# A recurrent and attention block with its modulation moved beside matrix products, paired attention heads, and split top-k lists

## What is computed

```python
# first block: three branches, joined by one product
o = rms_norm(o, norm_g) * silu(z)                  # delta rule, 8 heads of 128
z5 = gelu(y_s5)                                    # state space, 512 channels
y_s5 = z5 * sigmoid(z5 @ s5_w_glu + b) * silu(s5_gate)
h = h + concat([y_rg, y_gdn, y_s5]) @ w_out        # 2048 -> 1024
gate = sigmoid(rms_norm(h, g) @ ple_w_gate)
h = rms_norm(h + gate * (p @ ple_w_proj), final_norm_g)
# delta rule, per chunk and head: a unit lower triangle is inverted
sol = triangular_solve(I + strict(K K^T * decay), rhs)
# modulation of two later layers, from a condition vector: scales, shifts and
# gates, one product of the condition with w_mod_2 (2 layers, 1024 x 6144)
# attention: 8 heads of 64 in two groups, each query block of 128 against three
# neighbouring key blocks and 256 context keys, with a sink in the softmax
# router of each expert layer: affinity = softmax(h @ w_router), 16 experts,
# and each expert takes its 128 highest tokens
```

## Time and profile before

| | us |
|---|---|
| three runs | 5097.38, 5098.56, 5117.61 |
| median | 5098.56 |
| the profiled execution (span 5129.8) | 5131.51 |

### The profile page before, as it was taken

How to read it: one execution, slowest core, us unless ns; L and a number is a source line. 1 busy time by engine, 2 the same in 40 slices (tenths; PEclk the granted TensorE clock), 3 DMA queues, 4 the chain that set the end, 5 groups by cost and what they waited for, 6 DMA issues and landing times. The chain is left out here.

```text
span 5129.8 us, 38618 instructions
## 1 busy us (share of the span) xinstructions
PE 4519.5 (88%) x14430; PEld 2352.2 (46%) x14430; DVE 1728.6 (34%) x3087; ACT 976.0 (19%) x1876; POOL 205.3 (4%) x235
## 2 busy tenths in 40 slices
PE   8999996586989699888687999997989995799996
PEld 3444443572444454558453444443444444344443
DVE  3545534554431331554544111112124245311111
ACT  3444431242010311351110000002000001000001
POOL 0011100000000000001000000000000000000000
PEclk9999998797989799897776999998999996899998
DMA  4122225356110121005237999972011112799995
GB/s 111 45 69 82 66 70 161 96 168 242 66 49 0 61 72 55 1 25 145 74 132 273 341 319 318 317 264 86 17 34 42 34 42 99 269 317 317 317 317 205
DMA packets 515952, 733.51 MB, mean 143 GB/s; under 512 B 114270, under 2 KB 228798, under 8 KB 515800
## 3 DMA queue, kind: packets, MB, share of 16 engines
q1 hardware_dynamic: 479032, 646.54, 37.0%
q0 software_dynamic: 11744, 43.00, 3.0%
q10 hardware_dynamic: 25024, 41.96, 2.3%
HBM read 655.40 MB, written 76.01 MB: 143 GB/s over the span
## 5 line engine op out<-in xcount | busy, mean ns | idle before, releaser
L2361 PE MATMUL ps<-ffn_w,moe_xT 128*128 128x512 f32 x2048 | 887.6, 594 | 3.3 <-DVE moe_xT L2422 3.3
L512 PE MATMUL ps<-hT,pr_w 128*128 128x512 f32 x1536 | 671.3, 595 | 5.0 <-issue 3.6
L2361 PEld LDWEIGHTS ps<-ffn_w,moe_xT 128*128 128x128 f32 x2048 | 390.3, 191 | 494.9 <-issue 490.8
L512 PEld LDWEIGHTS ps<-hT,pr_w 128*128 128x128 f32 x1536 | 290.6, 191 | 364.4 <-issue 361.7
L2377 PE MATMUL ps<-moe_w,moe_hT 128*128 128x512 f32 x1024 | 444.9, 592 | 0.1
L2435 DVE TENSOR_TENSOR moe_sg<-moe_sg,ps 128x512 f32<-128x512 f32 x64 | 44.0, 688 | 836.7 <-PE ps L2361 836.7
L2377 PEld LDWEIGHTS ps<-moe_w,moe_hT 128*128 128x128 f32 x1024 | 192.1, 190 | 230.1 <-issue 230.1
L2769 PE MATMUL ps<-hA,abp_w 128*128 128x512 f32 (+1 forms) x624 | 252.3, 565 | 0.6 <-DVE bv L2882 0.6
L2576 PE MATMUL ps<-hG,gmu_w 128*128 128x512 f32 x512 | 227.7, 603 | 4.8 <-DMA gmu_w<-in_gm_w_in 4.8
L2492 PE MATMUL ps<-gmv_w,hG 128*128 128x512 f32 x512 | 222.3, 597 | 10.2 <-DMA gmv_w<-in_gm_w_in 10.2
L2402 ACT ACTIVATE moe_sg<-ps 128x512 f32<-128x512 f32 x64 | 38.2, 597 | 1006.9 <-PE ps L2361 1006.9
(11 more groups left out here) (608 smaller groups left out, 5764.7 us busy)
## 6 DMA issues: line engine op xcount, KB each, us to landing
ffn_w<-in_moe_w_gate SPq DMA_DIRECT2D x64, 2048.0 KB, 10.3
ffn_w<-in_moe_w_up SPq DMA_DIRECT2D x64, 2048.0 KB, 9.1
moe_w<-in_moe_w_down SPq DMA_DIRECT2D x64, 2048.0 KB, 10.5
pr_w<-in_w_in SPq DMA_DIRECT2D x24, 1024.0 KB, 5.4
X<-in_w_mod ACTq DMA_DIRECT2D x10, 2048.0 KB, 9.8
route_modw<-in_w_mod ACTq DMA_DIRECT2D x10, 2048.0 KB, 8.1
X<-scratch_grow SPq DMA_DIRECT2D x48, 256.0 KB, 5.3
X<-scratch_k SPq DMA_DIRECT2D x32, 256.0 KB, 3.5
```

What stands on the lines that cost most here:

```text
L512: ins = eng.matmul(C.ps[r % NRING][:, :], w[:, (n // 2) % NW, k, (n % 2) * P:(n % 2 + 1) * P], HT[:, k, half * BANK:(half + 1) * BANK], st ...
L2361: ins = eng.matmul(C.ps[2 + b][:, :], xT[:, k, :], wb[b][:, k, :], start=(k == 0), stop=(k == KD - 1))
```

## The change

- The second elimination of `stage_gdn` is put on GpSimd; DVE does the first alone. GpSimd's copies are put on ACT. SP stores the first inverse and goes on to the loads, and stores the second before unit 8.
- `stage_gdn_out` and `stage_s5_out` are one stage, `stage_outs`. The reciprocal root is taken on ACT as exp(-0.5 ln(x)); the reciprocal on DVE is gone.
- `Modulation` is gone. `ModColumns` sums w_mod's rows, scaled by the condition, on DVE (96 instructions for a layer with one condition, 128 with two for four blocks), from 48 loads of 512 KB with two buffers, and turns each block to channels by products with one moving column. Layer 1 runs inside `wout`, layer 0 inside `ple`. The bank it needs leaves 7 to `wout`, and three tiles instead of four in flight to `ple`.
- `stage_attn` takes both groups in one pass: score products of the two groups on PE's rows 0 to 63 and 64 to 127, value products on its columns 0 to 63 and 64 to 127, five phases per query block, the division two and the transposes three query blocks behind.
- `stage_route` makes the router's product with 512 moving columns for the two halves of the tokens side by side, runs the rounds on 64 partitions by 512 tokens, and merges the two sorted lists of each expert by a product with a reversed identity and the larger of each pair.

```diff
--- before.py
+++ after.py
...
+            eng.wait_ge(s_al[1], 16)
+            step = Steps(eng, s_iv1)
+            for j in range(B - 1):
+                eliminate(eng, step, 1, j)
...
+            inverse_store(0)
             for u in range(4):
                 inverse_load(u)
             for u in range(4, NU):
+                if u == HU:
+                    inverse_store(1)
                 inverse_load(u)
                 rec_load(u)
...
+                eng.activation(X5[g][0:32, :, 32:64], AT[u][0:32, :, 32:64], ACT.Copy)
+                eng.activation(X5[g][64:96, :, 96:128], AT[u][64:96, :, 96:128], ACT.Copy).then_inc(s_X5, 1)
+
+            x5(0)
+            x5(1)
+            transposed(0)
...
+def stage_outs(nc, C, A, S, MIX, X):
...
+            def root(h):
+                r = rt[:, h % 2, :]
+                if h >= 2:
+                    eng.wait_ge(s_n, h - 1)
+                for half in range(2):
+                    eng.wait_ge(s_ss, 2 * h + half + 1)
+                    eng.activation(rt[:, h % 2, half_(half)], ssb(h, half), ACT.Ln, bias=C.eps[:, 0:1], scale=1.0 / P).then_inc(s_ln, 1)
+                eng.wait_ge(s_ln, 2 * h + 2)
+                eng.activation(r, r, ACT.Exp, scale=-0.5).then_inc(s_rt, 1)
...
+            square(0)
+            square(1)
+            for t in range(ST_):
+                gelu(t)
+            for h in range(HEADS):
+                root(h)
+                if h + 2 < HEADS:
+                    square(h + 2)
+                if h == HEADS // 2:
+                    eng.wait_ge(s_par, 32)
+                    sigmoid(0)
+                    sigmoid(1)
+            sigmoid(2)
+            sigmoid(3)
...
+            for h in range(5):
+                squares(h)
+            eng.wait_ge(s_w, 16)
+            eng.wait_ge(s_z, ST_)
+            glu(0)
+            glu(1)
+            for h in range(5, HEADS):
+                squares(h)
+            glu(2)
+            glu(3)
...
+class ModColumns:
+        for i in range(SHARE * KD // KQ):
+            u, kq = divmod(i, KD // KQ)
+            if i >= 2:
+                eng.wait_ge(self.s_used, i - 1)
+            eng.dma_start(self.parts[:, i % 2, :, :], A["w_mod_2"][l][kq * KQ * P:(kq + 1) * KQ * P, u * BANK:(u + 1) * BANK]
+                          .rearrange("(k p) c -> p k c", p=P)).then_inc(self.s_w[i % 2], 16)
...
+    def sums(self, eng):
+
+        for i in range(SHARE * KD // KQ):
+            u, kq = divmod(i, KD // KQ)
+            if u >= 2 and kq == 0:
+                eng.wait_ge(self.s_turned, u - 1)
+            eng.wait_ge(self.s_w[i % 2], 16 * (i // 2 + 1))
+            for k in range(KQ):
+                for r in range(self.rows(u)):
+                    w, a, c = self.parts[:, i % 2, k, :], self.acc[:, u % 2, r, :], self.C.cond[:, kq * KQ + k, r:r + 1]
+                    if kq == 0 and k == 0:
+                        ins = eng.tensor_scalar(a, w, c, None, ALU.mult)
+                    else:
+                        if r == 0 and k:
+                            eng.wait_ge(self.s_chain, i * (KQ - 1) + k)
+                        elif r == 0:
+                            eng.wait_ge(self.s_used, i)
+                        ins = eng.scalar_tensor_tensor(a, w, c, a, ALU.mult, ALU.add)
+                    if r == self.rows(u) - 1:
+                        ins.then_inc(self.s_chain if k < KQ - 1 else self.s_used, 1)
+                    yield
...
+    def turn(self, eng, u):
+
+        eng.wait_ge(self.s_used, KD // KQ * (u + 1))
+        n = BANK // P
+        for r in range(self.rows(u)):
+            for i in range(n):
+                o = (u * n + i) * 2 + r
+                ins = eng.matmul(self.C.ps[7][:, o:o + 1], self.acc[:, u % 2, r, i * P:(i + 1) * P], self.C.ones[:, 0:1], start=True, stop=True)
+        ins.then_inc(self.s_turned, 1)
...
+                    if md and 2 <= u < SHARE + 2:
+                        md.turn(eng, u - 2)
...
+                    if md and u < SHARE + 2:
+                        for _ in range(16 if u < 4 else 8):
+                            next(side, None)
+                    if md and u == SHARE + 2:
+                        md.finish(eng)
...
+PACE = (0, 2, 2, 2, 2, 2, 2)
...
+        nbk = 7 if md else 8
+        bank = lambda p, t: C.ps[(TH * p + t) % nbk][:, :]
...
+            def free(p, t):
+                q, t0 = divmod(TH * p + t - nbk, TH)
+                if q >= 0:
+                    eng.wait_ge(s_acc, nacc[q] + (t0 + 1) * len(SEVEN[q][2]))
...
+                        if md and p and k == 2:
+                            md.turn(eng, 2 * p - 1)
+                        if md and k == 6:
+                            md.turn(eng, 2 * p)
...
+                    if p:
+                        aside(PACE[p])
...
+                if md and p + 2 == NP:
+                    aside(SHARE * KD * 2)
+                    md.finish(eng)
...
+            for k in range(KD):
+                for half in range(2):
+                    ins = eng.matmul(C.ps[0][EQ * half:EQ * (half + 1), :], wr[:, k, :], HT[:, k, half * BANK:(half + 1) * BANK],
+                                     start=(k == 0), stop=(k == KD - 1), tile_position=(0, EQ * half))
...
             eng.wait_ge(s_t, 1)
-            for half in range(2):
-                step(eng.tensor_copy(affT[:, half * BANK:(half + 1) * BANK], C.ps[1 + half][0:E, :]))
+            step(eng.tensor_copy(affT[:, :], C.ps[2][0:HP, :]))
             for r in range(RND):
                 v8 = vals[:, 8 * r:8 * r + 8]
                 step(eng.max(v8, affT[:, :]))
                 step(eng.max_index(ixu[:, 8 * r:8 * r + 8], v8, affT[:, :]))
-                step(eng.match_replace(affT[:, :], v8, affT[:, :], -1.0))
+                if r + 1 < RND:
+                    step(eng.match_replace(affT[:, :], v8, affT[:, :], -1.0))
             eng.tensor_copy(ixf[:, :], ixu[:, :]).then_inc(s_top, 1)
...
+            eng.tensor_copy(lists[:, :, :], C.ps[3][:, 0:2 * HP].rearrange("p (a e) -> p a e", a=2)).then_inc(s_ls, 1)
+            eng.wait_ge(s_ls, 1)
+            eng.wait_ge(s_rv, 1)
+            near, nid = lists[:, 0, 0:E], lists[:, 1, 0:E]
+            fval, fid = C.ps[4][:, EQ:EQ + E], C.ps[4][:, HP + EQ:HP + EQ + E]
+            eng.tensor_tensor(won[:, :], near, fval, ALU.is_ge).then_inc(s_rv, 1)
+            step(eng.tensor_copy(idx[:, :], won[:, :]))
...
+                if x:
+                    for g in range(2):
+                        eng.matmul(bank[g][:, at * P:(at + nb) * P], S.bq[row[g], x - 1, qs], S.bk[row[g], lo * P:(lo + nb) * P],
+                                   start=True, stop=True, tile_position=(D_ * g, 0))
+                    for g in range(2):
+                        ins = eng.matmul(bank[g][:, LOC:], S.bq[row[g], x - 1, qs], S.kc[row[g], 0:P],
+                                         start=True, stop=True, tile_position=(D_ * g, 0))
+                else:
+                    for h in range(GH):
+                        for g in range(2):
+                            ins = eng.matmul(bank[g][:, h * P:(h + 1) * P], S.bq[row[g], h, qs], S.kc[row[g], P:],
+                                             start=True, stop=True, tile_position=(D_ * g, 0))
...
+            def values(z):
+                n, x = zs[z]
+                eng.wait_ge(s_cp, 2 * z + 2)
+                if x == 0 and n:
+                    eng.wait_ge(s_po, n)
+                for g in range(2):
+                    cs = slice(D_ * g, D_ * (g + 1))
+                    ins = eng.matmul(C.ps[7][cs, :], S.bv[:, keys(n)[x][1], cs], PT[z % 4][:, g, :],
+                                     start=(x == 0), stop=(z + 1 == z_end[n]), tile_position=(0, D_ * g))
...
+            for n in range(NT + LAG):
+                for x in range(NPH):
+                    if n < NT:
+                        scores(n, x)
+                    z = z_of.get((n - LAG, x))
+                    if z is not None:
+                        turn(z)
+                        if z:
+                            values(z - 1)
+            values(len(zs) - 1)
...
+            for n in range(NT + LAG):
+                for x in range(NPH):
+                    if x == 0 and n < NT:
+                        context(n)
+                    if x and 1 <= n <= NT:
+                        exps(n - 1, (2 * x - 2, 2 * x - 1))
+                    z = z_of.get((n - LAG, x))
+                    if z is not None:
+                        copies(z)
+                        if x == 1 and n > LAG:
+                            outputs(n - LAG - 1)
...
-        stage_gdn_out(nc, C, A, S, MIX, X, mod, cond, 0, SHARE)
-        stage_s5_out(nc, C, A, S, MIX, X, mod, gains)
-        stage_seven(nc, C, "wout", MIX, plain_rows(A["w_out"][0], 16), 16, X)
+        stage_outs(nc, C, A, S, MIX, X)
+        stage_seven(nc, C, A, "wout", MIX, plain_rows(A["w_out"][0], 16), 16, X, extra=(S, mod, gains, SHARE, 0))
...
```

(4 more changed lines are left out.)

777 lines of the change are left out of this document (376 added, 401 removed).

## The result

Four executions of the changed kernel took 4956.81, 4961.62, 4950.05 and 4944.85 us, median 4953.43; four of the kernel before 5097.38, 5098.56, 5117.61 and 5097.47, median 5098.02. The ratio is 0.9707, 95% interval 0.9678 to 0.9736: faster by 145 us. In a later comparison of four executions with seven the medians were 4956.24 and 5108.50, ratio 0.9695 (0.9668 to 0.9723). Forecast were 4895 us and a range of 4850 to 4945, so the direction held and the time did not: it lies 58 us above the forecast and 8 above the range. The profiled execution of after took 4956.81 us (span 4955.1), 174.7 us of span less than that of before.

A forecast was written before the change was run, and what follows sets the result against it. Stages bound separately: PE in `wout`, `ple` and attention, DVE's top-k in routers, reciprocals and modulation loads in ends, idle PE in `stage_gdn`. Terms -23 -84 +35 +27 -42 -43 -73 = -203; 5098.6 - 203 = 4895 us, range 4850 to 4945.

The forecast's parts named there:

- Inverse: In `stage_gdn`, PE starts 23.4 us earlier after the first store, with GpSimd's half covered: gain 23 us.
- Ends: In the end stages, ACT carries the chain at 6.05 us a head, DVE covered: 84 us against 168.1, gain 84.
- The drain: Rival in the end stages: every table load also drains, adding 26 us, total 4921; chance 0.04.
- rival of one table for logarithm and exponential: Rival in the end stages: both functions share one table, saving ACT some 18 us, total 4877; chance 0.03.
- `wout`: Loss 35 us: turns 15, first block's wait 10, banks 4, changeovers 3, half clock 3; bounds 12 and 60.
- `ple`: Loss 27 us: 20 sets of turns 19, PE's waits in the first four blocks 5, tail 3; bounds 15 and 60.
- rival that the loads become the clock: Rival: w_mod loads pace `wout` and `ple`, biting from 3.7 us a part; time 5110 or more; chance 0.04.
- Attention: Paired products overlap, the bound passes to PE, DVE and ACT at about 17 us a block: 165 us, gain 42.
- the rival: In the attention, score products of both groups do not overlap: 19.5 us per block, total 4922; chance 0.12.
- the case of 18 us: In the attention, tiling mode changes at an assumed 0.2 us each: PE holds 18 us a block, some 8 longer.
- Routers: Shorter top-k rounds and product gain 43 us in each router; the first also loses the modulation, gaining 73.
- The step to the median: Profiled execution lay 33 us above the median, so only the difference was taken: 5098.6 - 203 = 4895 us.

The follow-up runs named there:

- the experiment that takes the cover away: Kernel after with square root on ScalarE and reciprocal on VectorE again in the merged end stage: stage 106.1 us, total 4993.62 us.
- the experiment with pairs: Kernel after with the end stage's roots taken in pairs of heads, eight table loads fewer: stage 74.9 us, total 4939.66 us.
- the second profile: The kernel before, unchanged, profiled once more: 5119.98 us.

## Why the prediction was right or wrong, step by step

- **Inverse, -23 forecast, -11: wrong.** The steps behind the store held (PE 5.1 us after the first load; GpSimd 0.55 us an instruction against 0.61, done at 940.8, covered). The step that failed is "so PE starts 23.4 us earlier" (it was 14.6: 938.44 against 953.03), which took for granted that DVE's own half costs what it cost alone. With GpSimd beside it an instruction took some 600 ns instead of 363; started one after the other, DVE's half is back at its old length and 10.2 us are gained. Another 3.0 us are ScalarE's transposing copy (a period of 22.0 instead of 19.0), which I had not placed: it stands at the one point of the period where PE waits for ScalarE. The Trainium skill has this rule ("SBUF — State Buffer", section "SBUF: two separate sides"): a VectorE instruction with two SBUF inputs and a GpSimd instruction that reads SBUF need the same pair of ports, and whichever comes second blocks for the other's whole instruction. The direction agrees with the rows; the size does not quite, since GpSimd was slowed by only 4% (26.4 us against 25.5), and work that takes each of them alone 25.5 and some 15 us (42 instructions at 363 ns) went through in 26.7 us. I had not weighed it.
- **Ends, -84 forecast, -83.3: right**, with the mechanism (5.89 us a head, nineteen loads, the first half of the product awaited: ScalarE's sigmoid waited 2.56 us for PE before 1164.5, forecast some 5). The reading that DVE is covered is borne out by the experiment that takes the cover away.
- **The drain** at a table load, a rival of 26 us: against it stood 0.02 us in the earlier trace rows, and the experiment with pairs settles it. Eight loads fewer brought 9.9 us, 1.24 each. The page "ScalarE: Activation LUTs" of the Trainium skill (section "What ACT_TABLE_LOAD costs") gives some 2.7 us for a load with its drain, from which I estimate 21 us for eight. The measurement decides: no drain shows here. The rival of one table for logarithm and exponential falls by the nineteen loads in the trace.
- **`wout`, +35 forecast, +30.3: right.** PE's busy time rose by 16.5 us, against 18 forecast for turns and half clock together, but in other parts: the turns are 12.3 (15 forecast), and the other products were busy 202.2 us instead of 194.6 (3 forecast). Its waits rose by 14: 9.7 for the first block (10 forecast) and 4.3 for banks and changeovers (4 and 3).
- **`ple`, +27 forecast, +41.8: the size was wrong.** Turns 16.5 us and tail 3.0 (5.2 behind PE's last product, 2.2 before) are near the 19 and 3; the "20 sets of turns" are 16, 128 one-column instructions of eight a set. The step that failed is "PE waits in their turns, 5 us together; the other eight take 9.4 against 9.8, covered". A part landed after 3.9 us, not 3.35, and PE waited 13.2 us in eight places. And I had put the half clock behind an idle stretch into the sum of `wout`, but not here, where the products became 9.1 us longer. The rival that the loads become the clock was given 0.04 as a disaster, but in small it was at work: two buffers cost `ple` 12.7 us.
- **Attention, -42 forecast, -33.1: the size was wrong.** The pairs overlap (the 152 value products took 42.6 us against 81.8, the scores 58.2 against 98.7), so the rival falls. The work in a block was read rightly: PE 15.7 us (15.1 and some more forecast), DVE 15.4 (15.8), ACT 13.6 (14.5). So the price of a change of tiling, 15 in a block, is small, and not the 0.2 us assumed for the case of 18 us. The step that failed is "So the bound passes from PE to all three, at about 17 per block": the engines do not only load each other, they wait for each other once a block, PE for the last shares and DVE for the scores behind them, which made 18.8. Two moves, one in DVE's list and one in ScalarE's, brought 17.2 and then 15.8. By parts: the first two blocks took 19.8 us against 29, the other six and the tail 152.5 against 136. One of the six took 24.3, with PE partly at half clock (0.86 granted). The forecast also has a slip: 205.4 - 165 is 40.4, not 42.
- **Routers, -43 and -73 forecast, -43.4 and -71.5: right.** Rounds of 2.29 us (2.28), the product 9.4 (9).
- **The step to the median: wrong in its assumption.** I took the difference, -203, off the median although the profiled execution lay 33 us above it, "with no single stage to blame". The stage to blame in part is the mLSTM stage, which cannot be seen in one profile. The first profile had it long, and its touched stages were some 6 us longer than in the second. Of the two profiled executions of before 5131.5 lies above all others (5097 to 5122) and 5120.0 near their upper end. The true terms with my base would still have given 5098.6 - 170 = 4928, 25 us too little. Set against the second profile they are -164; against seven further executions the difference is -152. The second profiles of both lie 153 apart, with after's mLSTM stage 10 us longer than before's. But nothing shows that it is usually longer in after, so the last 12 us stay open: no profile shows the mLSTM stage of an execution in the middle of before's range.
